# Three of nine input tiles scaled by GpSimd instead of VectorE, in a one-layer hybrid decoder step

## What is computed

```
def rmsnorm(x, g):
    y = xf * lax.rsqrt(jnp.mean(xf * xf, axis=-1, keepdims=True) + EPS)
    return (y * g.astype(jnp.float32)).astype(x.dtype)

xn = rmsnorm(x, norm_mix)
proj = xn @ w_in                 # 1024 -> 5888
...                              # dilated attention, gated convolution, gates, w_o
x = x + jnp.square(jax.nn.relu(rmsnorm(x, norm_mlp) @ w_ff1)) @ w_ff2
```

## Time and profile before

| | |
|---|---|
| median of the runs | 1674.63 us |
| the profiled execution | 1675.57 us, of which the span from first to last instruction is 1673.8 us |
| TensorE busy | 1640.2 us, 98% of the span |
| VectorE busy | 687.7 us, 41% |
| ScalarE busy | 482.6 us, 29% |
| GpSimd busy | 79.1 us, 5% |
| granted TensorE clock, mean | 0.998 of full speed |

### The profile page before, as it was taken

How to read it: one execution, slowest core, us unless ns; L and a number is a source line. 1 busy time by engine, 2 the same in 40 slices (tenths; PEclk the granted TensorE clock), 3 DMA queues, 4 the chain that set the end, 5 groups by cost and what they waited for, 6 DMA issues and landing times. The chain is left out here.

```text
span 1673.8 us, 28340 instructions
## 1 busy us (share of the span) xinstructions
PE 1640.2 (98%) x10667; PEld 1588.5 (95%) x10667; DVE 687.7 (41%) x1236; ACT 482.6 (29%) x925; POOL 79.1 (5%) x94
## 2 busy tenths in 40 slices
PE   7999999999989999999999999999999999999997
PEld 7899998899978999999999999999999999999997
DVE  6112123334644444333644353333333333333566
ACT  5212123443433443112323320133102320133223
POOL 0150000000000000000121000000000000000021
PEclk9999999999999999999999999999999999999999
DMA  5444564242267876342111111111111111111224
GB/s 164 129 122 131 167 191 124 84 132 80 76 171 185 197 184 174 128 127 70 48 50 38 50 38 50 45 43 41 47 50 38 50 38 50 38 51 38 63 69 152
DMA packets 237202, 155.87 MB, mean 93 GB/s; under 512 B 23982, under 2 KB 227590, under 8 KB 237146
## 3 DMA queue, kind: packets, MB, share of 16 engines
q1 hardware_dynamic: 208590, 124.00, 26.5%
q10 hardware_dynamic: 26268, 28.31, 5.0%
q0 software_dynamic: 2288, 2.80, 0.8%
HBM read 122.00 MB, written 35.43 MB: 94 GB/s over the span
## 5 line engine op out<-in xcount | busy, mean ns | idle before, releaser
L647 PE MATMUL bank<-xhi,wh 128*128 128x352 f32 (+1 forms) x1104 | 372.0, 337 | 4.1 <-DVE xlo L1577 2.0
L648 PE MATMUL bank<-xlo,wh 128*128 128x352 f32 (+1 forms) x1104 | 360.3, 326 | 0.0
L649 PE MATMUL bank<-xhi,wl 128*128 128x352 f32 (+1 forms) x1104 | 359.8, 326 | 0.0
L1123 ACT ACTIVATE wh<-wr 128x1024 fp32r<-128x1024 f32 (+1 forms) x142 | 144.6, 1018 | 432.4 <-PE bank L649 336.4
L1539 DVE TENSOR_TENSOR wl<-wr,wh 128x1024 fp32r<-128x1024 f32 (+1 forms) x142 | 181.6, 1279 | 189.0 <-ACT wh L1123 187.8
L648 PE MATMUL bank<-hlo,wh 128*128 128x368 f32 (+1 forms) x768 | 251.4, 327 | 0.0
L647 PE MATMUL bank<-hhi,wh 128*128 128x368 f32 (+1 forms) x768 | 250.6, 326 | 0.3 <-DVE rel L1963 0.3
L649 PE MATMUL bank<-hhi,wl 128*128 128x368 f32 (+1 forms) x768 | 250.1, 326 | 0.0
L647 PEld LDWEIGHTS bank<-xhi,wh 128*128 128x128 f32 x1104 | 207.4, 188 | 15.7 <-issue 7.6
L648 PEld LDWEIGHTS bank<-xlo,wh 128*128 128x128 f32 x1104 | 207.6, 188 | 0.0
L649 PEld LDWEIGHTS bank<-xhi,wl 128*128 128x128 f32 x1104 | 207.5, 188 | 0.0
(11 more groups left out here) (235 smaller groups left out, 2053.9 us busy)
## 6 DMA issues: line engine op xcount, KB each, us to landing
wr<-in_w_ff_dram SPq DMA_DIRECT2D x72, 512.0 KB, 3.9
wr<-in_w_in_dram SPq DMA_DIRECT2D x46, 512.0 KB, 4.2
d_T<-stg ACTq DMA_DIRECT2D x18, 544.0 KB, 2.8
kvc<-in_cache_kv_g_dram SPq DMA_DIRECT2D x16, 512.0 KB, 6.3
kvc<-in_cache_kv_g_dram SPq DMA_DIRECT2D x32, 256.0 KB, 7.2
d_tm<-tm ACTq DMA_DIRECT2D x12, 512.0 KB, 3.7
d_m<-bb ACTq DMA_DIRECT2D x8, 544.0 KB, 3.2
ml<-d_m SPq DMA_DIRECT2D x8, 544.0 KB, 4.1
```

Source lines behind the costliest of these rows:

```text
L647: pe.matmul(bank[c][:, 0:n], wh[st_.p][:, k, :], a, start=(k == 0), stop=False)
L648: pe.matmul(bank[c][:, 0:n], wh[st_.p][:, k, :], b, start=False, stop=False)
L649: last = pe.matmul(bank[c][:, 0:n], wl[st_.p][:, k, :], a, start=False, stop=(k == nk - 1))
L1123: act.activation(wh[st_.p][:, 0:nk, :], wr[st_.p][:, 0:nk, :], ACT.Copy).then_inc(w_hi, 1)
```

## The change

Tiles 2, 5 and 8 are scaled by GpSimd, in two instructions: first by the norm weights `gb`, as soon as the tile's squares have been summed (so that ScalarE no longer reads it), then by the root of its rows, as soon as VectorE has it. The two have a semaphore between them. VectorE's three `scale_x` calls for these tiles go, and TensorE waits for a GpSimd semaphore where it turns one of the three.

```
+POOL_TILES = (2, 5, 8)
...
         def turn_x(t):
             w = rows_of(t)
-            pe.wait_ge(x_scaled, t + 1)
+            if t in POOL_TILES:
+                pe.wait_ge(x_scaled_p, POOL_TILES.index(t) + 1)
+            else:
+                pe.wait_ge(x_scaled, t + 1 - sum(u < t for u in POOL_TILES))
...
         scale_x(1)
         split_x_lo(0)
-        scale_x(2)
...
         split_x_lo(3)
-        scale_x(5)
...
         split_x_lo(6)
-        scale_x(8)
...
+        pool.wait_ge(gb_c, 2)
+        for n, t in enumerate(POOL_TILES):
+            w = rows_of(t)
+            pool.wait_ge(x_sq, t + 1)
+            pool.tensor_tensor(xt[0:w, t, :], xt[0:w, t, :], gb[0:w, :], ALU.mult).then_inc(x_weighted, 1)
+            pool.wait_ge(x_weighted, n + 1)
+            pool.wait_ge(rs_d, 5 * n + 10)
+            pool.tensor_scalar(xt[0:w, t, :], xt[0:w, t, :], rst[0:w, 4, t:t + 1], None, ALU.mult).then_inc(x_scaled_p, 1)
+
         pool.wait_ge(bt_st, 16)
```

More of the change, by code:

```diff
@@ L282, in build @@
     x_sq, rs_d, rs_a = sem("x_squares"), sem("rstd_by_dve"), sem("rstd_root")
-    x_scaled, x_pe, x_hi, x_lo = sem("x_scaled"), sem("x_turned"), sem("x_hi"), sem("x_lo")
+    x_scaled, x_scaled_p, x_weighted, x_pe, x_hi, x_lo = sem("x_scaled"), sem("x_scaled_by_pool"), sem("x_weighted_by_pool"), sem("x_turned"), sem("x_hi"), sem("x_lo")
     stg_a = sem("stage_prompt_tail")
```

## The result

The changed kernel takes 1679.02 us (median of 13 runs, 1677.66 to 1682.49) where the kernel before takes 1674.91 on the same chip (median of 13). The ratio is 1.0026, with a 95% interval from 1.0017 to 1.0034: slower, by about 4.1 us by the medians. Forecast were 1678.7 us and a range of 1675.8 to 1683.0. The profiled execution took 1678.69 us, its span 1676.9.

A forecast was written before the change was run, and what follows sets the result against it. TensorE, almost without gaps from about 20 us, bounds the kernel, so only the start counts: 1.35 + 1.63 + 1.4 - 0.3 = 4.1 us on the profiled 1675.57 gives 1679.7, by the median 1678.7; range 1675.8 to 1683.0.

The forecast's parts named there:

- ScalarE's chain: Start, tiles 1 and 2: GpSimd's product of tile 2 holds VectorE's root, so tile 1's high part comes 1.35 us late.
- the two-column step: First step of VectorE's root of tiles 1 and 2, held by GpSimd's product; if not held, ScalarE's term is 0.73 us.
- The root of tiles 3 to 5: GpSimd's product of tile 5 holds VectorE's first two-input step of this root: 1.63 us more before tile 3's turn.
- Tile 4: GpSimd's second instruction for tile 5 goes before the weights' split; TensorE waits 0.55 us, not counted beside the clock loss.
- the rule that who waits gets the next turn: Of GpSimd and VectorE instructions that stop each other, the later one waits and then gets the next turn.
- The clock: TensorE's stop before tile 3 grows from 1.02 to about 3.3 us; the clock falls and charges 1.4 us.
- The 0.30 of tile 5's scaling: Tile 5's scaling leaves VectorE ahead of low parts that the product at 31.93 waits for: -0.30 us.
- tile 8 held nobody: GpSimd's product of tile 8 falls between 27 and 31 us, beside low parts, and holds nobody.
- The code load: GpSimd's first product needs its code, asked for at about 2.3 us; taken as done before 10.25, costing nothing.
- rival 2: Code load or second instruction at its upper bound makes GpSimd the bound: sum 4.6 or 5.9; late load 1681 to 1683; chance 0.17.
- Rival 3: Small steps and scaling pass GpSimd unhindered; only the 0.30 remains: 1674.3 us, not slower; chance 0.13.
- rival 1: The clock stays, or the two-column step is not held: 1677.2 to 1677.9 us; chance 0.22.

The follow-up runs named there:

- the scalar instruction alone: Kernel before, all scalings on VectorE; GpSimd only makes three of the second instructions into a tile nobody reads: 1675.1 us against 1673.83 (1.0008).
- dummy products: Changed kernel with twelve more dummy products in TensorE's stop before tile 3: 1678.15 us against 1674.14 for the kernel before (1.0018).
- the repeat of the kernel before: Kernel before run and profiled once more, no edit: 1673.68 us against 1674.02 (0.9998).
- the fills against the product: Kernel before plus GpSimd work on a tile nobody reads: three pairs of fills, 1674.46 us against 1673.91; three products, 1678.09 against 1673.83.

## Why the prediction was right

1. **ScalarE's chain, forecast 1.35 late, measured 1.96.** The mechanism is as forecast up to the high part of tile 1 (1.25 late), the two-column step held included. The other 0.6 us is the mis-sized term: GpSimd's second instruction. I took 1.30 us with an upper bound of 2.40, the price of the product, and it takes 2.85 by its rows: in the one for tile 2 (no row shows it with nobody in the way) it stands until the scaling of 13.58 has read its last, about 14.74 (0.12 before that row's end, much as in the prediction's reading of the earlier trace rows), and ends at 17.59. So tile 2 comes from GpSimd 1.18 us late for TensorE, and ScalarE stands 0.60 for it. The bound was wrong because one input was taken to cost no more than two. The Trainium skill (GPSIMD Engine Reference, 4.1 Engine selection) puts one input at roughly line rate, from which the prediction had estimated 1.0 us; the measurement decides.
2. **The root of tiles 3 to 5, forecast 1.63, measured 1.63** (1.79 less 0.16), and the tile turned 1.34 behind the start of its scaling, as before. With the row above this makes 3.58 instead of 2.98.
3. **Tile 4.** Forecast was a split of the weights that waits for GpSimd. It went first, at 1.22, here and with the scalar instruction alone; the scaling behind it was held instead, by 0.78. So the rule that who waits gets the next turn, read from the overlaps before, does not hold for GpSimd's second instruction, and this step of the prediction was wrong. The scaling was ready at 29.00, and TensorE, slowed by the clock, did not wait for it. With the clock kept up it loses 0.25 us there (3.11 us from turn to turn instead of 2.86) where 0.55 were forecast.
4. **The clock, forecast 1.4, measured 1.37** (4.95 less 3.58); with dummy products 1.12 of it is regained. But the reason given, that a stop of 1.99 us does no harm and one of 2.46 does, does not hold: the repeat of the kernel before fell at 1.99 us, and the changed one did not at 2.46.
5. **The 0.30 of tile 5's scaling came back** (4.95 to 4.62); tile 8 held nobody, as forecast: the scaling that stands at 36.28 beside its scalar instruction takes 1.27.
6. **The code load** cost nothing.

The sum in the start is 4.62 instead of 4.1, by the 0.6 us of the first point; 4.6 is what rival 2 gave for a second instruction at its upper bound. The medians differ by 4.1, and by the interval of the ratio the loss is 2.8 to 5.7 us, so the times can't tell the two sums apart; the hit to 0.3 us in the median is partly luck. Rival 3 (nothing stops) is excluded by the fills against the product, rival 1 by the two-column step of 2.33 and the window at 0.50. Of rival 2 the slow second instruction happened, at 0.6 us, and the late code did not. So the main mechanism is the forecast one, with this part of rival 2 in it.

Open is what lets the weights' split pass ahead of a scalar instruction of GpSimd that has waited since before, while a waiting product gets its turn ahead of the same split. Open too is why the runs of one kernel scatter by 2 to 6 us: falls of the clock like those seen, at 1 to 2 us each, could make much of it, but no run shows each one's. Some of it arises far behind the start: the repeat of the kernel before, 0.71 us later at the second chunk, is 0.69 earlier at the stop near 1643.

## What to carry to other kernels

Before work is moved to an idle GpSimd, look which VectorE instructions will lie beside it, and of those at the small ones on the critical path: here a step of 0.16 us stood for most of a GpSimd product of 2.37 us. Ask of the engine that sets the path whether it loses any work at all; here ScalarE set it and lost none, and of the three scalings taken from VectorE only 0.30 us came back. Sum such a loss from instruction starts in the stage itself, since single executions of one kernel differ elsewhere by microseconds.

## What the runs showed of the hardware that was not expected

- A product with one number per row of 128x1024 float32 takes GpSimd 2.85 us by the rows, longer than the product of two tiles (2.40). It holds a scaling of VectorE's for only 0.78 us of that (2.06 against 1.28), in its first part, and a scaling that comes 1.2 us into it runs free (1.27 at 36.28). The product holds VectorE to within 0.03 us of its end.
- GpSimd's product of 64 rows takes as long as that of 128 (2.39), and of a tile by itself 1.90.
- Whether the clock falls in a stop differs between executions of one kernel. In the stop of 2.46 us at the end of the kernel, the window from 1640 us shows 0.83 before and 1.00 in its repeat and after. After a stop of 1.99 us it stayed up in one profile and fell in another.
